# A two-layer attention and MLP trunk on one core: first weights in pieces on ScalarE's queue, shared angles, a rewritten layer head, and masks as the moving operand

## What is computed

```python
def hybrid_layer(x, ...):
    h = rms_norm(x, g_mix_pre)
    (c_q, c_kv, k_rope, q_swa, k_swa, v_swa, q_sb, k_sb, v_sb, gate_logits) = split(h @ w_in)
    o_a = mla_branch(c_q, c_kv, k_rope, ...) @ w_o_mla      # 8 heads, causal, softmax
    o_b = swa_branch(q_swa, k_swa, v_swa, ...) @ w_o_swa    # 8 heads, window 128, sinks, rotary
    o_c = stick_breaking_branch(q_sb, k_sb, v_sb) @ w_o_sb  # 8 heads, strictly causal
    gates = sigmoid(gate_logits + b_gate)
    mixed = gates[0] * o_a + gates[1] * o_b + gates[2] * o_c
    x = x + rms_norm(mixed @ w_out, g_mix_post)
    h = rms_norm(x, g_mlp_pre)
    return x + rms_norm(square(relu(h @ w_up)) @ w_down, g_mlp_post)

def mla_branch(c_q, c_kv, k_rope, ...):      # c_q has 256 channels, c_kv 128
    q = rms_norm(c_q, g_q_lat) @ w_uq        # 8 heads x (64 + 32 rotary)
    kv = rms_norm(c_kv, g_kv_lat) @ w_ukv    # 8 heads x (64 key + 64 value)
```

## Time and profile before

| | |
|---|---|
| median of 3 runs | 1829.33 us |
| the profiled execution's own time | 1829.59 us |
| its span, first to last instruction | 1827.8 us |
| TensorE matmul busy | 1769.8 us (97%) |
| VectorE, ScalarE, GpSimd busy | 1073.2 (59%), 823.2 (45%), 145.8 us (8%) |
| mean granted TensorE clock | 0.992 |

### The profile page before, as it was taken

How to read it: one execution, slowest core, us unless ns; L and a number is a source line. 1 busy time by engine, 2 the same in 40 slices (tenths; PEclk the granted TensorE clock), 3 DMA queues, 4 the chain that set the end, 5 groups by cost and what they waited for, 6 DMA issues and landing times.

```text
span 1827.8 us, 21093 instructions
## 1 busy us (share of the span) xinstructions
PE 1769.8 (97%) x8380; PEld 1455.5 (80%) x8380; DVE 1073.2 (59%) x1397; ACT 823.2 (45%) x1102; POOL 145.8 (8%) x140
## 2 busy tenths in 40 slices
PE   6899999999999999999999999999999999999996
PEld 5688888888877888888777888888888788888884
DVE  7787776664537534354496777755554565343545
ACT  5566565564335423231355755555544354232211
POOL 0011121110200000000001111211111000000000
PEclk9999999999999999999999999999999999999998
DMA  4122111222332222222221221122224232232221
GB/s 147 51 66 70 58 58 63 68 68 81 115 115 81 93 93 94 99 96 93 92 94 61 66 70 59 47 70 70 70 81 131 76 104 92 93 104 93 92 94 69
DMA packets 46466, 152.32 MB, mean 83 GB/s; under 512 B 5280, under 2 KB 7456, under 8 KB 46368
## 3 DMA queue, kind: packets, MB, share of 16 engines
q1 hardware_dynamic: 45216, 148.87, 24.8%
q10 hardware_dynamic: 1152, 2.10, 0.3%
HBM read 146.75 MB, written 4.19 MB: 83 GB/s over the span
## 4 chain that ended last, share of the span: by engine, by line
PE 87%; DVE 7%; ACT 3%; issue 1%; DMA 1%; POOL 0%; SPq 0%; DVEq 0%; ACTq 0%
PE bank L453 79%; PE bank L458 5%; DVE w_lo L1316 1%; PE bank L701 1%; PE bank L634 1%; PE bank L660 1%; DVE hf L1366 1%; DVE x L1373 1%; ACT w_hi L845 1%; DVE h_lo L1355 1%; DMA raw<-in_w 0%; DVE rst L1333 0%; PE bank L522 0%; POOL mxr L1962 0%; DVE rstd L1336 0%
## 5 line engine op out<-in xcount | busy, mean ns | idle before, releaser
L453 PE MATMUL bank<-h_hi,w_hi 128*128 128x512 f32 x1248 | 492.4, 395 | 22.8 <-DVE h_lo L1355 21.8
L453 PE MATMUL bank<-h_lo,w_hi 128*128 128x512 f32 x1248 | 487.4, 391 | 0.0
L453 PE MATMUL bank<-h_hi,w_lo 128*128 128x512 f32 x1248 | 487.2, 390 | 0.0
L845 ACT ACTIVATE w_hi<-raw 128x1024 fp32r<-128x1024 f32 (+2 forms) x278 | 280.1, 1012 | 227.9 <-DMA raw<-in_w 227.5
L1316 DVE TENSOR_TENSOR w_lo<-raw,w_hi 128x1024 fp32r<-128x1024 f32 (+2 forms) x278 | 328.2, 1183 | 64.4 <-ACT w_hi L845 58.1
L453 PEld LDWEIGHTS bank<-h_hi,w_hi 128*128 128x128 f32 x1248 | 235.2, 188 | 75.5 <-DVE w_lo L1316 16.2
L453 PEld LDWEIGHTS bank<-h_hi,w_lo 128*128 128x128 f32 x1248 | 235.0, 188 | 50.0
L453 PEld LDWEIGHTS bank<-h_lo,w_hi 128*128 128x128 f32 x1248 | 235.2, 188 | 48.1 <-issue 1.4
L453 PE MATMUL bank<-u_hi,w_hi 128*128 128x512 f32 x512 | 201.7, 394 | 0.0
L453 PE MATMUL bank<-u_lo,w_hi 128*128 128x512 f32 x512 | 201.7, 394 | 0.0
L453 PE MATMUL bank<-u_hi,w_lo 128*128 128x512 f32 x512 | 201.7, 394 | 0.0
(11 more groups left out here) (240 smaller groups left out, 2580.5 us busy)
## 6 DMA issues: line engine op xcount, KB each, us to landing
raw<-in_w SPq DMA_DIRECT2D x260, 512.0 KB, 3.3
x<-in_x SPq DMA_DIRECT2D x16, 256.0 KB, 3.3
x_spill<-x ACTq DMA_DIRECT2D x8, 256.0 KB, 2.0
x<-x_spill SPq DMA_DIRECT2D x8, 256.0 KB, 3.3
out_y<-x SPq DMA_DIRECT2D x8, 256.0 KB, 2.0
raw<-in_w SPq DMA_DIRECT2D x8, 192.0 KB, 2.7
raw<-in_w SPq DMA_DIRECT2D x8, 128.0 KB, 2.3
cst_f<-in_const SPq DMA_DIRECT2D x1, 640.0 KB, 9.3
```

Of the source, the lines that this page charges most:

```text
L453: mm = pe.matmul(o, s, m, start=start and i == 0 and j == 0, stop=last and i == n - 1 and j == 2, skip_group_check=True)
L845: act.activation(w_hi[:, gc % RING, 0:w], raw[:, gc % RING, 0:w], ACT.Copy).then_inc(whi.sem, 1)
```

## The change

1. **Start.** The first three weight chunks no longer come whole on SyncE's queue. ScalarE's queue issues the positions, the angle parameters and then the three chunks in four pieces by channel tile (`FIRST`: t 0, t 1, t 2-3, t 4-7, each a piece of all three chunks); SyncE's queue issues the vectors, all eight x tiles, chunk 3 and the constants. The pieces are split by `first_high` and `first_low` between the x tiles, and `three_tiles` waits for them piece by piece. VectorE first sets part of `cst` to ones, and TensorE runs 14 matmuls on them before its first tile. ScalarE, not VectorE, copies the constants; `x_square_sum` in layer 0 comes after latent tile 3, not in its middle.
2. **Tables.** Four tables and three angle sets at the start become tables from two angle sets: signs go into the sine's scale (`table_sign` is gone), and the rotary key needs one product with a table for all 128 rows.
3. **Head.** Epsilon is added into the sums of squares (`EPS_ROW`), so `mean_square`, `eps_x` and the two `ms2` operations go, and each Newton step reads the PSUM sum. The two latents' 1/rms are separate, so queries can start when two latent tiles are split. The keys of heads 0 and 1 and the first three `mla_v` tiles get banks of their own (`APART`), and the fourth `mla_v` comes after `mla_scores(0)`. The maximum of head 0 is taken before the value splits.
4. **Masks.** The masks (stored transposed) are the moving operand and the identity the stationary one, one add for each bank: 3 instead of 4 for a head of branch one and three, 6 instead of 14 for two heads of the window branch.
5. **Norms.** `norm_refine` has one VectorE operation less.

```diff
+FIRST = [(0, 1), (1, 2), (2, 4), (4, 8)]
+APART = [("mla_k", 0)] + [("mla_v", j) for j in range(NB - 1)]
+G = {tile: k for k, tile in enumerate(tile for tile in T if tile not in SIDE + APART)}
...
+        def v_bank(j):
+            return (bank[5], bank[7], pv_bank, tile_bank(("mla_v", NB - 1)))[j]
+        def first(buffer, i):
+            a, b = FIRST[i]
+            return buffer[:, 0:3, a * P:b * P]
...
                 sp.dma_start(vec_all[:, :], A_vec).then_inc(vec_loaded, 16)
-                sp.dma_start(x[:, 0, :], A_x[:, 0, :]).then_inc(x_loaded[0], 16)
-                sp.dma_start(pos_i[:, :], A_pos.broadcast_to([P, SEQ])).then_inc(angles_loaded, 16)
-                sp.dma_start(trig[:, :], A_trig).then_inc(angles_loaded, 16)
-                for gc in range(DEPTH * CHUNKS):
+                for t in range(KT):
+                    sp.dma_start(x[:, t, :], A_x[:, t, :]).then_inc(x_loaded[t], 16)
+                for gc in range(3, DEPTH * CHUNKS):
...
+                        if pieces and t in (0, 1, 2, 4):
+                            pe.wait_ge(first_lo, (0, 1, 2, 4).index(t) + 1)
...
+                def causal_mask(to, off, b, mask):
+                    if b == 1:
+                        return add(to[:, off:off + SEQ].rearrange("p (j q) -> p j q", q=P)[:, 0:NB:NB - 1, :],
+                                   cst[:, IDENT, :], cst[:, mask:mask + 1, :].broadcast_to([P, 2, P]))
+                    return add(to[:, off:off + P], cst[:, IDENT, :], cst[:, mask, :])
...
-                        for i, m in enumerate(masks[:w // P]):
-                            mm = add(to[:, off + col + i * P:off + col + (i + 1) * P], cst[:, m, :],
-                                     cst[:, IDENT, :])
                         if n + 1 == len(pieces) or pieces[n + 1][3] != b:
-                            mm.then_inc(score_full.sem, 1)
+                            causal_mask(to, off, b, MASK_CAUSAL).then_inc(score_full.sem, 1)
...
+                            both = cst[:, MASK_CAUSAL:MASK_PREV + 1, :].rearrange("p a c -> p (a c)")
+                            for r in range(2):
+                                if b == 0:
+                                    mm = add(band[r][0][:, :].rearrange("p (a c) -> p a c", a=2), cst[:, IDENT, :],
+                                             both.unsqueeze(1).broadcast_to([P, 2, 2 * P]))
+                                else:
+                                    add(band[r][1][:, 0:2 * P], cst[:, IDENT, :], both)
+                                    mm = add(band[r][1][:, 2 * P:3 * P], cst[:, IDENT, :], cst[:, MASK_CAUSAL, :])
...
+                pe.wait_ge(ones_set, 1)
+                keep_warm(13)
+                pe.matmul(bank[2][:, :], cst[:, ONE, :], cst[:, 0:4, :], start=True, stop=True,
+                          skip_group_check=True).then_inc(warmed, 1)
...
-                    for j in range(NB):
+                    for j in range(NB - 1):
                         mla_v(j)
                     mla_scores(0)
+                    mla_v(NB - 1)
                     mla_q(1)
...
+                act.dma_start(pos_i[:, :], A_pos.broadcast_to([P, SEQ])).then_inc(angles_loaded, 16)
+                act.dma_start(trig[:, :], A_trig).then_inc(angles_loaded, 16)
+                for i, (a, b) in enumerate(FIRST):
+                    act.dma_start(first(raw, i), A_w[0, 0:3][:, :, a * P:b * P].rearrange("c p k -> p c k"))\
+                       .then_inc(first_loaded[i], 16)
                 act.preload_act_table_set(LN_EXP)
...
-                    act.wait_ge(*ms_set(4))
-                    guess(2, rs02[:, :, :], ms2[:, :, :], 0.0, 1.0, rst2[:, :, :])
+                    split(6)
+                    act.wait_ge(*sum_all(2))
+                    guess(2, rs02[:, 0, :], bank[5][:, :], 0.0, 1.0 / Q_LORA, rst2[:, 0, :])
+                    act.wait_ge(*sum_all(3))
+                    guess(4, rs02[:, 1, :], pv_bank[:, :], 0.0, 1.0 / KV_LORA, rst2[:, 1, :])
```

More of the change, by code:

```diff
@@ L20 @@
 THETA = 10000.0
+EPS_ROW = EPS * 1024 / 128
 KT = D // P
@@ L272, in trunk @@
         x_loaded = [sem(f"x_loaded{t}") for t in range(KT)]
+        first_loaded = [sem(f"first_loaded{i}") for i in range(len(FIRST))]
+        first_hi, first_lo = sem("first_hi"), sem("first_lo")
+        ones_set, warmed = sem("ones_set"), sem("array_warmed")
+        const_set = sem("const_set")
         angle_set = sem("angle_set")
@@ L503, in three_tiles @@
                 def three_tiles(names, ready):
+                    pieces = names[0][0] == "latent" and not now[0]
                     for name in names:
-                        pe.wait_ge(*wlo(C[name] + 1))
+                        if not pieces:
+                            pe.wait_ge(*wlo(C[name] + 1))
                         take_bank(name)
@@ L1059, in _ @@
                 act.preload_act_table_set(LN_EXP)
                 act.wait_ge(vec_loaded, 16)
-                act.wait_ge(x_loaded[0], 16)
-                next_in(0, vec(V_PRE, layer=0))
-                x_square(0)
-                for c in range(3):
-                    split(c)
-                for t in range(1, KT):
+                for t in range(KT):
                     act.wait_ge(x_loaded[t], 16)
                     next_in(t, vec(V_PRE + t, layer=0))
-                    x_square(t)
@@ L1070, in _ @@
-                split(3)
-                for n in range(3):
-                    table_sin(n)
+                    if t < 3:
+                        first_high(t)
+                    if t:
+                        x_square(t - 1)
+                    if t == 3:
+                        first_high(3)
+                act.wait_ge(first_hi, len(FIRST))
+                act.sem_inc(whi.sem, 3)
+                x_square(KT - 1)
+                split(3)
+                table_sin(1, tab[:, 3, :], 3, slice(HEAD, P))
@@ L1682, in _ @@
+                    dve.scalar_tensor_tensor(out=csq[:, 2, :], in0=xsq[:, 0, :], scalar=EPS * KV_LORA / D, in1=csq[:, 2, :],
+                                             op0=ALU.mult, op1=ALU.add).then_inc(c_sum.sem, 1)
                     split(4)
-                    mean_square(1, 1)
-                    dve.tensor_scalar(eps_x[:, :], ms[:, :], EPS, None, ALU.mult).then_inc(ms_set.sem, 1)
+                    if not now[0]:
+                        dve.wait_ge(setup_act, 3)
+                        step(dve.memset(tab[0:HEAD, 2, :], 1.0))
@@ L1711, in _ @@
[L1711 to L1718 removed]
+                    dve.tensor_tensor(tmp[:, :], tab[:, 3, :], rstd_x[:, :], ALU.mult).then_inc(kr_part.sem, 1)
@@ new lines, in _ @@
+                    dve.wait_ge(*kr_part(1))
+                    dve.tensor_tensor(rb[:, :], kr_bank[:, :], tmp[:, :], ALU.mult).then_inc(free_of(("latent", 3)), 1)
+                    dve.wait_ge(*rs_square(2))
+                    newton(1, bank[5][:, :], Q_LORA, rs02[:, 0, :], rst2[:, 0, :], rstd2[:, 0, :])
+                    split(5)
+                    split(6)
+                    latent_scaled(0)
+                    latent_scaled(1)
+                    dve.wait_ge(*rs_square(3))
+                    newton(2, pv_bank[:, :], KV_LORA, rs02[:, 1, :], rst2[:, 1, :], rstd2[:, 1, :])
@@ new lines, in _ @@
+                    latent_lo(0, cqn_lo[:, 0, :], cqn_hi[:, 0, :])
+                    latent_lo(1, cqn_lo[:, 1, :], cqn_hi[:, 1, :])
+                    latent_scaled(2)
+                    scaled(("gate", 0, 0), mix[:, 0, :])
+                    latent_lo(2, ckn_lo[:, :], ckn_hi[:, :])
+                    split(7)
+                    dve.wait_ge(*freed(("latent", 3)))
+                    dve.tensor_tensor(ra[HEAD:P, :], rb[0:HEAD, :], rb[HEAD:P, :], ALU.add).then_inc(kr_sum.sem, 1)
+                    mla_q(0)
@@ L1721, in _ @@
                                       ALU.subtract).then_inc(kr_lo.sem, 1)
+                    mla_qk(0)
                     scaled(("gate", 0, 1), mix[:, 1, :])
-                    split(C["gate", 0, 1] + 2)
-                    mla_q(0)
-                    mla_qk(0)
-                    for j in range(NB):
-                        mla_v(j)
                     split(C["mla_v",] + 2)
                     mla_biggest(0)
+                    mla_v(NB - 1)
                     mla_q(1)
                     mla_qk(1)
+                    for j in range(NB - 1):
+                        mla_v(j)
                     split(C["gate", 0, 2] + 2)
```

284 lines of the change are left out of this document (139 added, 145 removed).

## The result

The changed kernel takes 1810.92 us (median of 4 runs, 1810.74 to 1811.1) against 1829.27 (1828.99 to 1829.69) for the kernel before in the same session: ratio 0.99, 95% interval 0.9882 to 0.9917, 18.4 us less. Forecast were 1798.5 and a range of 1793 to 1805: the sign was right, the gain was 18.4 in place of 30.8.

A forecast was written before the change was run, and what follows sets the result against it. TensorE was taken as the bound, its matmuls busy 1769.8 of 1827.8 us. Start 8.5, heads 4.8 and 7.1, masks 9.5 and norms 0.9 sum to 30.8 us off 1829.59, forecast 1798.5 after adjusting to the median, range 1793 to 1805.

The forecast's parts named there:

- the fourth piece: Start: the last weight piece, 786 KB, lands at about 14 us; 0.8 us charged for t = 4 and the step behind.
- the first pieces are late: Start, rival: short rows get the smaller share, piece 0 lands at 9, the fourth at 17.5; total 1803; chance 0.12.
- ScalarE's two table loads, sines and constant copy: Layer 0 head: about 6 us of ScalarE work, ending just about when latent tile 0 does, so no wait.
- would be the same: Start: its sum goes by bytes ahead of the piece, so loads from two queues sharing DMA engines would not change it.
- 2.5 us for the clock kept: Start: 14 matmuls on ones keep TensorE's higher clock level at the first real matmul; 2.5 us gained.
- TensorE is not held by VectorE in these stages, so this passes through.: Branches, masks: the gain from fewer mask adds, taken as 9.5 us, reaches the kernel's time.
- The masks' worth on TensorE: Branches: 3.4 us in one and three, 0.85 x 8 pairs = 6.8 in the window branch; sum 10.2, taken as 9.5.
- The head of layer 0: Start of layer 0: 8.0 us of waits and lower clock go, 3.2 of new waits come; 4.8 us gained (2.5 to 7).
- The head of layer 1: Start of layer 1: waits and lower clock of 9.0 us go, new waits 0.8 and 1.1; 7.1 us gained (5 to 8.5).
- The norms: Four norms, one VectorE operation of 0.69 us less in each: 0.9 us gained in all (0.2 to 1.4).
- The first matmul: Start: the first real matmul comes at 9.4 us, 6.8 us before the earlier 16.23.
- start: Start of the kernel: 6.8 + 2.5 - 0.8 = 8.5 us gained (5.5 to 10).

The follow-up runs named there:

- experiment 1: The changed kernel, with SyncE waiting for the fourth piece before it issues chunk 3 and the constants; 1808.55 us.
- experiment 9: The changed kernel, still with two queues, but the three chunks in two pieces of 768 KB with rows of 2 KB; 1808.81 us.
- experiment 8: The changed kernel with the four pieces on SyncE's queue, each behind its x tile; 1804.05 us.
- experiments 2 and 3: The changed kernel with 20 and with 1 matmuls on ones in place of 14; 1809.44 us and 1810.82 us.
- experiment 14: The changed kernel with one queue, rope input before the split in the window branch, 32 bytes of padding, and one matmul on ones in place of 14; 1800.12 us.
- experiments 4 and 5: The old masks in the changed kernel, 1816.66 us; the new masks alone in the kernel before, 1822.86 us.
- experiment 5: The kernel before with the new masks and nothing else; 1822.86 us.

## Why the prediction was wrong, step by step

**Wrong: the fourth piece.** "All of x and the pieces are 3.7 MB, 9.1 us at 406 GB/s, so it lands at about 14." It landed at 18.42. Two things failed in this step. I left chunk 3 and the constants out of the bytes (experiment 1: 2.3 us at the latents' end). And I let the two queues share as if the whole came in order; with short rows ScalarE's queue gets 26% (experiment 9), so x tiles that nobody needs yet go first (experiment 8: 5.4 us, which contains the 2.3). The rival "the first pieces are late" had this mechanism, with 17.5 for the last piece, and priced it at 3.3 to 5.8 us; 6.4 were lost. I gave it 0.12. Its other mark, a first piece at 9, did not come: that was 7.71.

**Wrong: "ScalarE's two table loads, sines and constant copy (...) end just about when latent tile 0 does. No wait there."** The work was sized right (6.2 us, from 25.9 to 32.14) and the wait put at nothing. ScalarE's list from the last piece's split to the first `cf` is 13.7 us without a gap, and tile 3 starts 14.46 us after that split begins. By my own terms tile 3 was due at 26.6 (9.4 + 72 x 0.2275 + 0.8); with the piece at 14 these 14.46 us put it at 28.5. Experiment 8, with the piece at 13.00, shows it: TensorE waits 0.81 us for `cf`. What moving the constants or the sines behind `cf` would give was not tried.

The Trainium skill's rules that I had quoted ("DMA: Bandwidth & Descriptors", sections "Issuing engines are not separate DMA queues" and "Queues, rings and completion order") agree with what was measured: a second issuer brought no bandwidth (3.82 MB by 14 us against 3.86 with one), and short rows got the smaller part (26% against 41%). By the first of them I had concluded that the sum "would be the same", and that was the mistake: bytes in order is only what one queue does.

**Wrong: 2.5 us for the clock kept.** The level fell at 9.6 in the changed kernel, and experiments 2 and 3 show that neither the level nor the matmuls on ones change the start of tile 3: the last piece and ScalarE's work behind it are the bound. With one queue (experiment 14) TensorE is close to that bound, and without the matmuls on ones the latents end 0.6 us later.

**Wrong: "TensorE is not held by VectorE in these stages, so this passes through."** The masks' worth on TensorE was well sized: 1.08 a pair (0.85 forecast) times 8, and 0.11 a head pass (0.105), about 11 us against 9.5 to 10.2. But 4.1 turned into waits for `ra`, `rp_lo` and `of`, and layer 0 had one fall more of the clock (1.5), which is chance as far as the runs tell. There was 0.2 us of slack at `ra` and 0.7 at `of`, and that rows of before could have told. That the shorter masks bring these waits is shown from both sides (experiments 4 and 5). That a second bank for the values would take away those for `of` is not tried.

**Not seen: the address.** 2.3 us in all, 1.4 of them in the two MLPs.

**Right.** The head of layer 0: 4.6 (4.8), with new waits of 0.70, 1.52 and 0.68 where 0.8, 1.3 and 1.1 were forecast, and none before `cqn_hi`. The head of layer 1: 7.3 (7.1), with 0.91 and 0.53 where 0.8 and 1.1 were forecast. A part of both rests on falls of the clock that the profile of before happened to have: in experiment 5, with the head of layer 0 as before but for the masks, the granted clock lacks 3.4 us of full speed there in place of 1.7, and that head takes 0.7 us more. They answer to the earlier trace rows:

```profile
47.36 0.50 PE L472 MATMUL bank<-h_hi,w_hi 128*128 128x512 f32 x1 [0.70 <-DVE w_lo L1377]
59.11 0.47 PE L472 MATMUL bank<-mq_hi,mk_hi 128*128 128x512 f32 x1 [1.52 <-issue]
64.35 0.47 PE L472 MATMUL bank<-h_hi,w_hi 128*128 128x512 f32 x1 [0.68 <-DVEq L1521]
...
950.89 0.47 PE L472 MATMUL bank<-mq_hi,mk_hi 128*128 128x512 f32 x1 [0.91 <-issue]
955.97 0.47 PE L472 MATMUL bank<-h_hi,w_hi 128*128 128x512 f32 x1 [0.53 <-DVEq L1521]
```

The norms: 0.34 each, 1.0 in all (0.9). The first matmul: 9.62 (9.4).

The shortfall adds up: start 6.4, new waits 4.1, clock 1.5, addresses 2.3, less the masks' 1.5 above forecast and 0.3 on heads and norms, is 12.5; 12.4 were missing. With the order of the loads, the address and the wait for `ra` put right the kernel is at 1800.4, 2 us from the forecast; the waits for `of` and `rp_lo` are still in it.

## What to carry to other kernels

Where loads feed a pipeline in a known order, put them on one queue in that order; here a second queue brought no bandwidth and let later bytes overtake, the more so with short rows in what was needed first. Then ask what the engine that prepares the data still has on its list behind the last arrival. Before counting fewer matmuls as gain, read how long ahead of TensorE the slower engine finishes at each hand-over of that stage: 0.2 us of slack pays out 0.2. When a small buffer changes its size, look where the later ones come to stand: here 32 bytes cost 2.3 us.
